# Eight conditioning chunks: from TensorE in the first attention to row sums in two feed-forwards

## What is computed

```python
mod_x = (jax.nn.silu(c) @ w_ada[l] + b_ada[l]).reshape(bn, 1, N_MOD, d)
mod_c = (jax.nn.silu(c_ctx) @ w_ada[l] + b_ada[l]).reshape(1, 1, N_MOD, d)
...
h_x = _half_ffn(h_x, norm_g[l, 0], mod_x[:, :, 0], mod_x[:, :, 1], mod_x[:, :, 2], ffn1_up[l], ffn1_down[l])
a_x = _modulate(_rmsnorm(h_x, norm_g[l, 1]), mod_x[:, :, 3], mod_x[:, :, 4])
```

## Time and profile before

| | us |
|---|---|
| median of 3 runs | 2090.39 (2090.31 to 2090.72) |
| the profiled execution, its own time | 2089.81 |
| its span, first to last instruction | 2088.5 |
| PE busy | 2062.4 (99%) |
| PE weight loads busy | 1766.4 (85%) |
| DVE busy | 1256.4 (60%) |
| ACT busy | 809.4 (39%) |
| POOL busy | 56.9 (3%) |
| DMA | 303.35 MB, 145 GB/s over the span |

### The profile page before, as it was taken

The page is one execution under the profiler, slowest core; times in us unless marked ns, Lnnn a source line. Parts: engine busy times, 40 slices in busy tenths (PEclk is TensorE's granted clock), DMA queues, the critical chain, the costliest instruction groups (busy, mean ns, idle before and its releaser), DMA issues.

```text
span 2088.5 us, 35023 instructions
## 1 busy us (share of the span) xinstructions
PE 2062.4 (99%) x14950; PEld 1766.4 (85%) x14950; DVE 1256.4 (60%) x1841; ACT 809.4 (39%) x1183; POOL 56.9 (3%) x58
## 2 busy tenths in 40 slices
PE   8999999999999999999999999999999999999998
PEld 8986899998888888867788888888888888889998
DVE  6766765766565536776755655465454446867665
ACT  6433543553222234356532222343222234365444
POOL 0000300000000000310000000000000000200000
PEclk9999999999999999999999999999999999999999
DMA  8627755454344324310333543233354325415543
GB/s 340 220 97 255 251 189 185 169 184 142 126 166 149 127 84 129 108 61 1 122 129 121 188 148 119 84 142 121 126 187 151 119 83 134 149 62 182 181 171 113
DMA packets 95676, 303.35 MB, mean 145 GB/s; under 512 B 14384, under 2 KB 53680, under 8 KB 74800
## 3 DMA queue, kind: packets, MB, share of 16 engines
q1 hardware_dynamic: 95536, 301.34, 42.1%
HBM read 300.26 MB, written 1.05 MB: 144 GB/s over the span
## 4 chain that ended last, share of the span: by engine, by line
PE 90%; DVE 6%; ACT 2%; issue 1%; DMA 1%; SPq 0%; ACTq 0%; DVEq 0%
PE ps L544 25%; PE ps L546 25%; PE ps L545 25%; DVE w_lo L531 2%; PE ps L2634 2%; PE ps L2371 1%; PE ps L2679 1%; PE ps L2699 1%; DVE a_lo L1655 1%; PE ps L576 1%; ACT a_hi L1504 1%; DMA raw<-in_w_in 1%; DVE nrm L1666 0%; PE ps L749 0%; ACT w_hi L525 0%
## 5 line engine op out<-in xcount | busy, mean ns | idle before, releaser
L544 PE MATMUL ps<-a_hi,w_hi 128*128 128x512 f32 (+2 forms) x2136 | 729.9, 342 | 3.3 <-DVE w_lo L531 1.9
L545 PE MATMUL ps<-a_lo,w_hi 128*128 128x512 f32 (+2 forms) x2136 | 725.3, 340 | 0.0
L546 PE MATMUL ps<-a_hi,w_lo 128*128 128x512 f32 (+2 forms) x2136 | 725.2, 340 | 0.0
L531 DVE TENSOR_TENSOR w_lo<-raw,w_hi 128x2048 fp32r<-128x2048 f32 (+1 forms) x227 | 468.2, 2065 | 121.0 <-ACT w_hi L525 120.5
L525 ACT ACTIVATE w_hi<-raw 128x2048 fp32r<-128x2048 f32 (+1 forms) x227 | 387.5, 1712 | 181.3 <-PE ps L546 170.7
L544 PEld LDWEIGHTS ps<-a_hi,w_hi 128*128 128x128 f32 x2136 | 404.5, 189 | 53.8 <-issue 7.0
L546 PEld LDWEIGHTS ps<-a_hi,w_lo 128*128 128x128 f32 x2136 | 404.5, 189 | 44.5
L545 PEld LDWEIGHTS ps<-a_lo,w_hi 128*128 128x128 f32 x2136 | 404.6, 189 | 43.7
L544 PE MATMUL ps<-ff_hi,w_hi 128*128 128x512 f32 (+1 forms) x880 | 306.5, 348 | 0.6 <-DVE ff_lo L1153 0.3
L545 PE MATMUL ps<-ff_lo,w_hi 128*128 128x512 f32 (+1 forms) x880 | 305.1, 347 | 0.0
L546 PE MATMUL ps<-ff_hi,w_lo 128*128 128x512 f32 (+1 forms) x880 | 305.0, 347 | 0.0
(11 more groups left out here) (457 smaller groups left out, 1947.1 us busy)
## 6 DMA issues: line engine op xcount, KB each, us to landing
raw<-in_w_gu SPq DMA_DIRECT2D x110, 1024.0 KB, 4.9
raw<-in_w_dn SPq DMA_DIRECT2D x80, 704.0 KB, 4.1
raw<-in_w_ada SPq DMA_DIRECT2D x36, 1024.0 KB, 5.7
row_w<-in_w_ada SPq DMA_DIRECT2D x72, 512.0 KB, 5.9
raw<-in_w_in SPq DMA_DIRECT2D x24, 1024.0 KB, 6.0
raw<-in_w_out SPq DMA_DIRECT2D x12, 1024.0 KB, 4.9
direct<-in_w_cmp SPq DMA_DIRECT2D x4, 1024.0 KB, 8.7
raw<-in_w_in SPq DMA_DIRECT2D x4, 512.0 KB, 7.7
```

The source lines that it names most:

```text
L531: nc.vector.tensor_tensor(w_lo[slot][:, cols], raw[b][:, cols], w_hi[slot][:, cols].bitcast(F32), ALU.subtract).then_inc(lo_ready if done ...
L544: nc.tensor.matmul(banks[m], w1, a1, start=start and k == 0, stop=False)
L545: nc.tensor.matmul(banks[m], w1, a2, start=False, stop=False)
L546: last = nc.tensor.matmul(banks[m], w2, a1, start=False, stop=stop and k == pr.kt - 1)
```

## The change

The eight chunks leave the first attention: `w_out` has no inner chunks, and no pair of the first attention carries one. The row sets of the first and the third 512-token feed-forward (`w_gu1_0`, `w_gu2_0`) grow from three to four, laid over all four products of the feed-forward instead of three (the second `w_dn` is new). The number of chunks stays 72, so each chunk number moves to another place. The gains of layer 0's attention norm are made one feed-forward later.

```diff
-INNER = {"w_out": (1, 8), "w_out_1": (2, 2), "w_gu": (2, 1), "w_gu1_0": (2, 1), "w_in_0": (2, 1),
+INNER = {"w_out_1": (2, 2), "w_gu": (2, 1), "w_gu1_0": (2, 1), "w_in_0": (2, 1),
          "w_gu2_0": (2, 1), "w_gu1_1": (2, 1), "w_in_1": (2, 1)}
...
-INNER_PAIRS = {"first": (0, 1, 2, 3), 0: (), 1: (2,)}
-ROWS = {"w_gu1_0": 12, "w_gu2_0": 12, "w_gu1_1": 12}
+INNER_PAIRS = {"first": (), 0: (), 1: (2,)}
+ROWS = {"w_gu1_0": 16, "w_gu2_0": 16, "w_gu1_1": 12}
...
-        for q in range(1, 3 if pr.rows else 0):
+        for q in range(1, 4 if pr.rows else 0):
             stage += range(products[i + q].base, products[i + q].end)
...
                 key = attend_key(pr)
-                if key == "first":
-                    inner_drain(dve, key, INNER_PAIRS[key][-1])
                 if key != "first":
...
-        flow += [("norm", f"{l}.0")] + (ffn[:-1] + [("mods", (1, 1))] + ffn[-1:] if l else ffn) + [("norm", f"{l}.1")] + take(1)
+        flow += [("norm", f"{l}.0")] + ffn[:-1] + [("mods", (l, 1))] + ffn[-1:] + [("norm", f"{l}.1")] + take(1)
...
-                dve_mods(dve, step, l, (n,) if l else (0, 1))
-                if l == 0:
+                dve_mods(dve, step, l, (n,))
+                if (l, n) == (0, 0):
```

## The result

| | before | after |
|---|---|---|
| median of 13 runs beside each other | 2089.77 us (2086.31 to 2090.72) | 2094.59 us (2092.28 to 2100.78) |
| ratio, 95% interval | | 1.0027 (1.0020 to 1.0034) |
| the profiled execution, its own time | 2089.81 | 2094.5 |
| its span | 2088.5 | 2093.2 |

The change makes the kernel slower, by 4.8 us in the medians (0.23%; by the ratio 0.27%, with an interval from 4.2 to 7.1 us) and 4.7 us in the two spans. I had forecast 0.7 us faster, and the time lies above my range of 2084.0 to 2094.0 us. In the changed kernel's trace the lines behind the deleted drain carry numbers lower by 2: L2846 is what was L2848, L2945 was L2947.

The account below looks back on a forecast made before the run. PE, busy 99% of the span, was taken to bound the kernel, with DVE setting the first attention's pace afterwards. Terms -1.5 - 1.6 + 2.4 = -0.7 us gave 2089.7 us from 2090.4, range 2084.0 to 2094.0.

Parts of the forecast that it names:

- Cost 0: Second w_dn product of each 512-token feed-forward: DVE's added row additions run 1.35 us late, within w_lo's 2.2 us slack, costing nothing.
- the case that the cover is gone: Feed-forward w_dn chunks: without w_lo's slack, DVE's lateness of 0.27 us a chunk would cost at most 2.7 us.
- my own sign of being wrong: Feed-forward: PE showing waits between 724 and 811 us would show the prediction wrong.
- The attention's gain: First attention: removing eight chunks gains 4.0 us, less 2.4 us for GpSimd's earlier work, leaving 1.5 us.
- The layout of the three engines: First attention: PE, DVE and ScalarE operations laid again in code order end at 228.0 us without chunks, gaining 4.0 us.
- GpSimd's price: First attention: GpSimd's earlier context squares slow DVE by 0.25 us an operation, 3.5 us less 1.1 of waiting, 2.4 us.
- my 14 operations: First attention, 208.7 to 221 us: DVE's four weighing operations of each of three jobs and two large ones, slowed by GpSimd.
- two neighbouring rows: DVE beside GpSimd: nearest profile rows show delays of 0.18 and 0.42 us an operation; 0.25 was taken, nearer the lower.
- the slow rival: First attention: each of 14 DVE operations waits for a whole GpSimd operation of 0.75 us; 2096.7 us, chance 0.10.
- The clock: First attention, a rival: new gaps on PE drop the clock to 0.50, costing 3.25 us; 2093.0 us, chance 0.05.
- The w_out stall: w_out stage: PE's 1.6 us wait for one w_lo goes once GpSimd has finished earlier, gaining 1.6 us.
- The two more sets on PE: The two feed-forwards: two added sets of row sums lie wholly on PE's path, costing 2.4 us.

Follow-up runs that it names:

- the kernel before with few squares: The kernel before, with only 3 of GpSimd's 15 operations on the squares of the context (that sum left incomplete): 2087.31 us, ratio 0.9991.
- The late sum's kernel: The changed kernel, with the fourth set's row sum on PE one chunk later: 2090.76 us, ratio 1.0002.
- the kernel with the early context load: The kernel before, with the load of the context half of h issued ahead of the sixth of the eight chunk loads: 2091.12 us, ratio 1.0011.
- the one with half of the chunks: The changed kernel, but four of eight chunks stay in the first attention, the others form one fourth set, its sum one chunk later: 2091.57 us, ratio 1.0006.

## Why the prediction was wrong

**The step that failed** is the term for the row additions on DVE, "Cost 0"; it measured +3.8 us. That DVE falls behind PE in the w_dn chunks, and that the next w_lo still comes in time (PE shows no wait for it there), was right. The size of the lateness came near by luck: 1.7 us at the fifth chunk (PE was ready at 794.14, the residual starts at 795.82) against my 1.35. I had 0.27 us a chunk, five times. In the changed kernel the residuals start at 765.52, 773.10, 780.67, 788.25 and 795.82 us, 7.57 us apart against PE's 7.48, so only 0.1 us is added a chunk; most of the lateness comes in at the first one, where DVE had 1.05 us of idle time before the change and not 2.21:

```profile
765.82 0.88 DVE L1228 SCALAR_TENSOR_TENSOR h<-ps,half_gate,h 128x256 f32<-128x256 f32 x2 [1.05 <-PE ps L546]
```

The failure is another one: I measured the lateness only against the w_lo's slack of 2.2 us. The row additions are the last thing that DVE does in a chunk, and PE has a reader for them too, the sum itself, which the plan places two chunks ahead of the eighth row's chunk. At no other sum does PE show a wait. The fourth set ends in the short w_dn chunks, where DVE finishes its last addition at 795.9 us and PE was ready at about 794.1. That gave 1.9 us twice; moving the sum one chunk later removes the wait and its 3.8 us with it. My bound for the case that the cover is gone, 2.7 us, priced the lateness of DVE and not the place of the reader, and so was too low as well. A wait of PE between 724 and 811 us was my own sign of being wrong, and it came.

**The attention's gain.** Forecast -1.5, measured -0.1. GpSimd began at 210.42 us (209 forecast), w_out at 232.70 (230.4 forecast). The layout of the three engines was right: 4.0 forecast, 3.8 measured once the squares are gone from it. What was mis-sized is GpSimd's price: 0.25 us an operation on 14, less 1.1, made 2.4 us; the trace has 0.36 us an operation, 5.0 in all, and 3.4 to 3.7 us came through to w_out. In my own sum, 14 x 0.36 - 1.1 = 3.9 us gives -0.1, as measured. I had picked my 14 operations partly wrong: the two large ones lost nothing (1.21 us each; the second starts at 223.02 us, behind the last square), the tiny multiplications by the gates lost up to 0.4. And I took the lower of two neighbouring rows because the weighing operations are short; they proved the most exposed of all, 1.14 us for four becoming 3.08.

The rule of the Trainium skill that I weighed there (SBUF — State Buffer, Who interferes with whom), an exclusive lock by which the second to come waits for the first to end, fits single rows of the traces well: a GpSimd operation that takes 0.61 us in most rows took 1.68 while DVE had a 1.21 us addition of two SBUF inputs running, started at the same instant, and an operation of DVE on 128x4 elements that starts 0.04 us behind one of GpSimd took 0.58 instead of 0.16, to the same end. As a price it is no better than my 0.25: the mean of 0.36 us an operation lies well below the slow rival's 0.75, and no run shows how long each single operation was held.

**The clock.** I gave the fall 0.05 and priced it at 3.25 us. It did fall in the attention of the changed kernel, for about 7 us, but cost 0.3 us: I had priced it as if PE set the pace there. Behind the attention's last gap, where PE is busy throughout, a fall of some 4 us went with 0.8 us in one pair of profiles.

**The w_out stall.** Forecast -1.6, measured -2.3 by the marks; its cause, GpSimd beside DVE, is shown by the kernel before with few squares. I had taken the one wait of 1.6 us for the whole price; its restart and the norm behind it carry the rest.

**The two more sets on PE.** Forecast +2.4, measured +2.5.

The sum with measured terms: -0.1 - 2.3 + 2.5 + 3.8 = +3.9 us (3.84 by the marks), of the 4.7 between the profiles; 0.9 lies ahead of the attention's second turn. In the medians the difference is 4.8, and the interval of the ratio (4.2 to 7.1 us) leaves out the 3.8, so the timed runs hold something that the marks behind the turn do not. It stays open. The late sum's kernel is at +1.35 us in the medians where its parts give -0.2; there the interval (-1.5 to +2.3 us) covers both.

## What to carry to other kernels

When work moves onto an engine with slack, check that slack against every reader of every result, not only the one that waits today: the moved work's own consumer may be the earliest. Work on GpSimd beside VectorE work from SBUF can cost: here 0.36 us for each of 14 VectorE operations where VectorE set the pace. A transfer that arrives earlier starts such work earlier; ask what wakes up with each transfer. And a gap that opens on the former bottleneck is worth only what the engine that takes over leaves.

## What the runs showed of the hardware

**DVE and GpSimd hold each other.** The timeline of POOL in the changed kernel shows it from the other side; the second DVE row under it starts at the same instant as the long row of POOL, the first one ends with the first of POOL:

```profile
210.42 0.61 POOL L3344 TENSOR_TENSOR ctx_sq<-h 128x256 f32<-128x256 f32 x1 [209.97 <-DMA h<-in_x]
...
213.29 0.72 POOL L3349 TENSOR_TENSOR ctx_sq<-ctx_sq,row_w 128x256 f32<-128x256 f32 x1
214.09 1.68 POOL L3344 TENSOR_TENSOR row_w<-h 128x256 f32<-128x256 f32 x1
```
```profile
210.46 0.58 DVE L2941 TENSOR_TENSOR fac<-fac,gt 128x4 f32<-128x4 f32 x1
...
214.09 1.21 DVE L2243 TENSOR_TENSOR p<-p 128x1024 f32<-128x1024 f32 x1
```

**The time's spread follows the clock.** In 27 timed executions of the kernel before on one chip the mean granted clock was 0.999 in nine (2087.97 us in the mean), 0.998 in fourteen (2089.89), 0.997 in three (2090.51) and 0.996 in one (2093.49). One place for it is seen: ahead of the attention the clock falls to 0.50 in some profiles and not in others, with the same work around it. First the kernel before, then the kernel with the early context load, both from 188 to 190 us:

```profile
188.00:190.00 2.00, 2.00 (x66) 1.94 (x66) 0.25 (x1) 1.59 (x3) 0.00 (x0) 0.50 0.93 375
```
```profile
188.00:190.00 2.00, 2.00 (x74) 1.65 (x74) 0.25 (x1) 1.96 (x3) 0.00 (x0) 1.00 0.97 385
```

The eight profiles with the fall reach the second turn at 202.49 to 204.28 us, the four without at 201.06 to 201.96. Seven of the eight are of the eight kernels in which all eight chunks moved, the other is the kernel before; the four without are one of those eight, the one with half of the chunks and two variants of the kernel before. These are few profiles, and on several chips, so whether the change makes the fall likelier is open. The timed runs would fit with it: the mean granted clock is 0.9956 over the thirteen of the changed kernel, 0.9964 over the eleven with the late sum, and 0.9979 to 0.9982 over the kernel before on three chips. The fall in the attention is part of that difference; what the rest costs no run isolates. A profile's lead or lag of 2 us at that mark can therefore not be read as a gain or loss of the edit behind it, and I would have misread the early context load's span of 2086.5 us as a gain without the timed runs (2091.12).
